# Levels issued in pairs in the recurrence phase, the last Fourier fold on GpSimd, and four smaller moves

## The reference

```python
def hybrid_mixer(h, w_in, w_fnet, lb_f, lb_b, out_norm, w_out):
    proj = h @ w_in                                    # 1024 -> 3072
    u, q, zf, zb, iv, g = jnp.split(proj, cuts, axis=-1)
    mixed = jnp.fft.fft2(ug, axes=(1, 3), norm="ortho").real      # 4 groups of 128
    y_fourier = jnp.einsum("blgc,gcd->blgd", mixed, w_fnet)
    k_f, logf_f = hgrn2_gates(zf, lb_f); k_b, logf_b = hgrn2_gates(zb, lb_b)
    o_fwd = chunked_gated_recurrence(qh, k_f, vh, logf_f)         # 4 heads of 128
    o_bwd = flip(chunked_gated_recurrence(flip(qh), flip(k_b), flip(vh), flip(logf_b)))
    y_rec = rms_norm(o_fwd + o_bwd, out_norm) * silu(g)
    return concatenate([y_fourier, y_rec]) @ w_out

def expert_choice_ffn(h, w_router, w_gate, w_up, w_down):
    affinity = softmax(xt @ w_router)
    g, idx = lax.top_k(affinity.T, cap)                # 16 experts, cap = tokens / 8
    he = silu(xe @ w_gate[e]) * (xe @ w_up[e]); ye = (he @ w_down[e]) * g
    return zeros.at[idx].add(ye)

x = x + hybrid_mixer(rms_norm(x, norm_mix), ...)
x = x + expert_choice_ffn(rms_norm(x, norm_ffn), ...)
return rms_norm(x, norm_final)
```

## Time and profile before

| what | us |
|---|---|
| median of 3 runs (2556.1 to 2558.35) | 2556.99 |
| the profiled execution's own time | 2552.32 |
| its span, first to last instruction | 2550.6 |
| PE busy in it | 2510.8 (98%) |
| DVE / ACT / POOL busy | 1648.6 (65%) / 1359.3 (53%) / 327.1 (13%) |
| mean granted TensorE clock | 0.997 |

### The profile page before, as it was taken

How to read it: one execution, slowest core, us unless ns; L and a number is a source line. 1 busy time by engine, 2 the same in 40 slices (tenths; PEclk the granted TensorE clock), 3 DMA queues, 4 the chain that set the end, 5 groups by cost and what they waited for, 6 DMA issues and landing times.

```text
span 2550.6 us, 44352 instructions
## 1 busy us (share of the span) xinstructions
PE 2510.8 (98%) x18109; PEld 2263.5 (89%) x18109; DVE 1648.6 (65%) x1997; ACT 1359.3 (53%) x1627; POOL 327.1 (13%) x237
## 2 busy tenths in 40 slices
PE   7999999999999999999999999999999999999998
PEld 6777778787877999999999999999999999999997
DVE  6556565444387676767667676766767666676667
ACT  6435353434665555555555555555555555555556
POOL 3102020101120011020211202021020202102020
PEclk9999999999999999999999999999999999999999
DMA  4001010135447676675767767676676767667677
GB/s 159 26 22 55 2 55 10 57 137 198 173 144 273 231 256 239 228 261 211 268 228 251 247 235 251 226 259 234 251 249 235 248 221 256 236 234 258 225 259 282
DMA packets 63987, 503.08 MB, mean 197 GB/s; under 512 B 7536, under 2 KB 7920, under 8 KB 39568
## 3 DMA queue, kind: packets, MB, share of 16 engines
q1 hardware_dynamic: 48016, 448.84, 48.3%
q0 software_dynamic: 15872, 52.83, 7.0%
HBM read 464.42 MB, written 37.22 MB: 197 GB/s over the span
## 4 chain that ended last, share of the span: by engine, by line
PE 92%; DVE 3%; ACT 2%; DMA 1%; issue 1%; POOL 0%; SPq 0%; DVEq 0%; ACTq 0%; POOLq 0%
PE up_banks_b L2241 15%; PE up_banks_a L2241 15%; PE up_banks_b L2244 6%; PE up_banks_a L2244 6%; PE bank L64 5%; PE bank L66 5%; PE bank L65 5%; PE up_banks_b L2282 2%; PE up_banks_b L2280 2%; PE up_banks_b L2281 2%; PE up_banks_b L2279 2%; PE up_banks_a L2283 2%; PE up_banks_b L2283 2%; PE up_banks_a L2279 2%; PE up_banks_a L2282 2%; PE up_banks_a L2280 2%
## 5 line engine op out<-in xcount | busy, mean ns | idle before, releaser
L2009 DVE TENSOR_TENSOR big_lo<-wide,big_hi 128x4096 fp32r<-128x4096 f32 x189 | 836.3, 4425 | 410.2 <-ACT big_hi L1774 410.0
L1774 ACT CAST big_hi<-wide 128x4096 fp32r<-128x4096 f32 x190 | 690.3, 3633 | 515.8 <-PE up_banks_a L2241 240.8
L2241 PE MATMUL up_banks_b<-x_parts,big_hi 128*128 128x384 f32 x2016 | 574.3, 356 | 0.0
L2241 PE MATMUL up_banks_a<-x_parts,big_hi 128*128 128x384 f32 x1984 | 565.0, 356 | 1.0 <-DVE h_parts L2033 1.0
L2244 PE MATMUL up_banks_b<-x_parts,big_lo 128*128 128x192 f32 x1764 | 442.0, 251 | 0.0
L2244 PE MATMUL up_banks_a<-x_parts,big_lo 128*128 128x192 f32 x1736 | 435.0, 251 | 0.0
L2241 PEld LDWEIGHTS up_banks_b<-x_parts,big_hi 128*128 128x128 f32 x2016 | 365.3, 189 | 0.2
L2241 PEld LDWEIGHTS up_banks_a<-x_parts,big_hi 128*128 128x128 f32 x1984 | 359.4, 189 | 1.9 <-DVE h_parts L2033 1.2
L2244 PEld LDWEIGHTS up_banks_b<-x_parts,big_lo 128*128 128x128 f32 x1764 | 336.1, 191 | 0.0
L2244 PEld LDWEIGHTS up_banks_a<-x_parts,big_lo 128*128 128x128 f32 x1736 | 330.8, 191 | 0.6
L64 PE MATMUL bank<-big_hi,w_hi 128*128 128x512 f32 x576 | 236.5, 411 | 0.0
(11 more groups left out here) (345 smaller groups left out, 4177.9 us busy)
## 6 DMA issues: line engine op xcount, KB each, us to landing
wide<-in_expert_weights SPq DMA_DIRECT2D x190, 2048.0 KB, 7.7
w_raw<-in_w_heads SPq DMA_DIRECT2D x48, 256.0 KB, 2.8
x_in<-in_x SPq DMA_DIRECT2D x12, 512.0 KB, 4.0
x_d<-in_x POOLq DMA_DIRECT2D x12, 512.0 KB, 5.8
residual<-x_d POOLq DMA_DIRECT2D x12, 512.0 KB, 3.6
ffn_in<-h_and_xT_d POOLq DMA_DIRECT2D x12, 512.0 KB, 3.0
wide<-residual SPq DMA_DIRECT2D x12, 512.0 KB, 6.4
tab<-in_tables POOLq DMA_DIRECT2D x10, 512.0 KB, 7.3
```

What stands on the lines that cost most here:

```text
L1774: nc.scalar.copy(ahead.hi(c), raw[:, c % RAW]).then_inc(hi_done, 1)
L2009: nc.vector.tensor_tensor(ahead.lo(c), raw[:, c % RAW], ahead.hi(c).bitcast(F32), ALU.subtract).then_inc(lo_done, 1)
L2241: last = nc.tensor.matmul(out[:, 0:2 * CAP], hi, x[:, k], start=n == 0, stop=n == KT - 1, skip_group_check=True)
```

## The change

1. **Heads, levels in pairs.** Levels 0 and 1, 2 and 3, 4 and 5, 6 and 7 are issued back to back on PE in the odd slots. For that the second level of a pair must not wait for a rise behind the first: a level with an even number reads copies of both its keys and its queries (`keys[0]` and the new buffer `queries`), an odd one a second buffer `keys[1]` and `kq`. ACT makes the copies in events of their own (`prep`), DVE rises once more as soon as they are made. Projections go into the slots as (1,2,1,2,1,2,1,0) halves, not (1,1,1,1,1,2,2,1): no half stands between level 7 and `intra`. The turn of v (`vt`) stands right before `intra`. `u` of the block before stands behind the half of slot 0 and directly ahead of the pair (0, 1). Updates and inters come one slot earlier; `rstd` moves to the front of its slot; where its `rows` stand at slot 7 they come behind `intra`. The copies of `near` into the scores are an event of their own (`near`) after `prep` of level 7.
2. **The last fold.** The sample's part of the fold of the last group goes from DVE to GpSimd (`fold_last`), behind GpSimd's last store of `u`.
3. **Kept sums.** ACT takes kept sums 0 and 1 behind the sixth of the eight w_out pieces, 2 behind the seventh and 3 behind the eighth.
4. **Weight piece.** The third early piece of L957 comes behind GpSimd's store of tile 10, not before that of tile 11.
5. **Prompt round.** Round 0 of the prompt's `take_best` goes from the end of the transform phase into the experts phase.
6. The program is built with `dynamic_dma_scratch_size=8192`.

```diff
+    BY_GPSIMD = (GROUPS - 1, 1)
+    def fold_rows(self, eng, on, g, part, done, count):
+        first, n = SEQS[part]
+        e, u = self.even[:, g, first // 2:(first + n) // 2], self.u[:, g, first:first + n]
+        on.tensor_copy(e[:, 0:1], u[:, 0:1]).then_inc(done, 1)
+        on.tensor_tensor(e[:, 1:], u[:, 1:n // 2], u[:, n - 1:n // 2:-1], ALU.add).then_inc(done, 1)
+        on.tensor_tensor(u[:, 1:n // 2], u[:, 1:n // 2], u[:, n - 1:n // 2:-1], ALU.subtract).then_inc(done, 1)
...
+    def fold_last(self, pool):
+        g, part = self.BY_GPSIMD
+        self.is_loaded(pool, g)
+        self.fold_rows(pool, self.nc.gpsimd, g, part, self.folded_last, 0)
...
-        keys = sb("keys", [P, BLK])
+        keys = [sb(f"keys{i}", [P, BLK]) for i in range(2)]
+        queries = sb("queries", [P, BLK])
...
-        FILL, LAST_FILL = (1, 1, 1, 1, 1, 2, 2, 1), (2, 2, 2, 1, 1, 1, 1, 1)
+        FILL, LAST_FILL = (1, 2, 1, 2, 1, 2, 1, 0), (2, 2, 2, 1, 1, 1, 1, 1)
...
-                    s = 1 + i // 2
+                    s = i // 2
                     at_slot[s] += [("update", h, d, k, turns[d][k]) for k in pair for d in range(2)]
                     at_slot[s + 1] += [("inter", h, d, k, turns[d][k + 1]) for k in pair for d in range(2)]
                 f = 2 + (steps - 1) // 2
                 at_slot[f] += [("square", h, b) for b in blocks]
                 at_slot[f + 1] += [("root", h, blocks[0])]
-                at_slot[f + 2] += [("rstd", h, blocks[0])]
+                at_front[f + 2] += [("rstd", h, blocks[0])]
...
             for s in range(8):
-                if n < NN:
-                    timeline.append(("level", n, s))
+                timeline += at_front[s]
+                if n < NN and s % 2 == 0:
+                    timeline.append(("prep", n, s + 1))
+                    if s == LEVELS - 1:
+                        timeline.append(("near", n))
+                elif n < NN:
+                    timeline += [("level", n, s - 1), ("level", n, s)]
+                    if s < LEVELS:
+                        timeline.append(("prep", n, s + 1))
+                if s:
+                    timeline += at_slot[s] + take_gates()
+                timeline += take_halves(FILL[s] if n < NN else LAST_FILL[s])
                 if s == 0 and n >= 1:
-                    timeline += [("u", n - 1, 0), ("u", n - 1, 1)]
-                timeline += at_slot[s] + take_gates()
-                timeline += take_halves(FILL[s] if n < NN else LAST_FILL[s]) + at_end[s]
+                    timeline += [("u", n - 1, 0), ("u", n - 1, 1)] + at_slot[0]
+                if s < 7 or n == NN:
+                    timeline += at_end[s]
             if n < NN:
-                timeline += [("intra", n), ("kt", n, 0), ("kt", n, 1)]
+                timeline += take_turn() + [("intra", n)] + at_end[7] + [("kt", n, 0), ("kt", n, 1)]
...
+                elif kind == "prep":
+                    _, n, s = ev
...
+                    if n >= 1 or s > 2:
+                        filled(act, ("level", n, s - 2) if s > 2 else ("level", n - 1, LEVELS + 1 - s))
+                    if s % 2 == 0:
+                        gather(queries, n, QB, QF, s - 1)
+                    gather(keys[s % 2], n, KF, KB, s - 1)
...
+                elif kind == "level" and ev[2] % 2 == 1:
                     _, n, s = ev
...
+                    rise(n, s)
+                    for t in (s - 1, s):
+                        take_level(("level", n, t))
+                elif kind == "prep" and ev[2] % 2 == 1 and ev[2] > 1:
+                    rise(ev[1], ev[2] - 1)
...
-    LOW_BETWEEN = {TT - 2: (0, 2), TT - 1: (4,)}
+    LOW_BETWEEN = {TT - 2: (0, 2)}
+    LOW_BEHIND = {TT - 2: (4,)}
...
-            act.wait_ge(wo_lo_done, KT)
-            for g in range(GROUPS):
+            def keep(g):
+                act.wait_ge(wo_lo_done, KT - 4 + g // 2 + 1)
                 act.wait_ge(y_filled, g + 1)
                 nc.scalar.copy(kept[:, g], banks[g][:]).then_inc(y_read, 1)
+            wo_high(range(KT - 2))
+            keep(0)
+            keep(1)
+            wo_high((KT - 2,))
+            keep(2)
+            wo_high((KT - 1,))
+            keep(3)
...
-            dve.wait_ge(aff_turned, 2)
-            take_best(then, nc, turned_lists, table, best, where, 2, 0, P_SLOTS)
+            ahead.aff_turned, ahead.turned_lists = aff_turned, turned_lists
...
-    nc = bacc.Bacc("TRN2", target_bir_lowering=False, num_devices=1)
+    nc = bacc.Bacc("TRN2", target_bir_lowering=False, num_devices=1, dynamic_dma_scratch_size=8192)
```

More of the change, by code:

```diff
@@ L495, in _ @@
                     pool.sem_inc(sig_used[i % 2], 1)
+            fourier.fold_last(pool)
         @block.scalar
@@ L512, in split_weights, with gather @@
                         weights.high(act, (h * NJ + j) * 2 + f)
-            def gather_keys(n, level):
-                if level == 0:
-                    act.wait_ge(kq_made, n + 1)
-                else:
-                    act.wait_ge(kq_up, n * LEVELS + level)
-                    filled(act, ("level", n, level))
-                if level == 0 and n >= 1:
-                    filled(act, ("level", n - 1, LEVELS))
+            def gather(out, n, left, right, level):
                 half = 1 << level
-                nc.scalar.copy(keys[:].rearrange("p (n two h) -> p n two h", two=2, h=half),
-                               halves(n % NB, KF, KB, level, 0, BLK)).then_inc(keys_ready, 1)
+                nc.scalar.copy(out[:].rearrange("p (n two h) -> p n two h", two=2, h=half),
+                               halves(n % NB, left, right, level, 0, BLK)).then_inc(keys_ready, 1)
             def take_projection(ev):
@@ L647, in sig_in, with rise, take_level @@
                 return sig[:, i % 2], sig_used[i % 2]
+            def rise(n, s):
+                nonlocal own
+                b, level = n % NB, s - 1
+                half = 1 << level
+                if level == 0:
+                    dve.wait_ge(kq_made, n + 1)
+                else:
+                    dve.wait_ge(kq_up, n * LEVELS + level)
+                pair = "p r (n two h) -> p r n two h"
+                products = decay[level][:].rearrange("p r (n two) -> p r n two", two=2)
+                shape = [P, 2, BLK // (2 * half), half]
+                right = kq[b][:, QF:KB + 1].rearrange(pair, two=2, h=half)[:, :, :, 1]
+                left = kq[b][:, KF:QB + 1].rearrange(pair, two=2, h=half)[:, :, :, 0]
+                up = decay[level + 1][:] if level + 1 < LEVELS else chunk_decay[:, b]
+                own += 1
+                nc.vector.tensor_tensor(up, products[:, :, :, 0], products[:, :, :, 1], ALU.mult).then_inc(dve_step, 1)
+                if s % 2 == 1:
+                    filled(dve, ("level", n, s))
+                else:
+                    prepared(dve, n, s)
+                own += 1
+                nc.vector.tensor_tensor(right, right, products[:, :, :, 0].unsqueeze(3).to_broadcast(shape), ALU.mult)\
+                    .then_inc(dve_step, 1)
+                nc.vector.tensor_tensor(left, left, products[:, :, :, 1].unsqueeze(3).to_broadcast(shape), ALU.mult)\
+                    .then_inc(kq_up, 1)
+            def take_level(ev):
+                _, n, s = ev
+                i = fill_of[ev][0]
+                if 1 <= s <= NEAR:
+                    filled(dve, ev)
+                    was_read(dve, ("level", n, s - 1))
+                    nc.vector.copy_predicated(near[:], mask[:, s - 1].unsqueeze(1).to_broadcast([P, CH, STRIP]),
+                                              near_view[i]).then_inc(bank_read[i], 1)
+                elif s == LEVELS:
+                    filled(dve, ev)
+                    dve.wait_ge(intra_done, n)
+                    nc.vector.tensor_copy(scores[P // 2:, :, 0:P // 2], bank[i][P // 2:, :, 0:P // 2])\
+                        .then_inc(bank_read[i], 1)
             norm.vector(dve)
@@ L1158, in _ @@
                     pool.dma_start(h_dram[row:row + P], h).then_inc(h_stored, 16)
+                    for k in ahead.LOW_BEHIND.get(s, ()):
+                        ahead.low_early(pool, nc.gpsimd, 1, slice(k, k + 2))
         @block.scalar
@@ L2055, in first_x_low @@
                     lows(r, first + r, hi_cols, lo_cols)
-            for slot in range(1, P_SLOTS):
-                take_best(choose, nc, table, table, best, where, 2, slot, P_SLOTS)
+            for slot in range(P_SLOTS):
+                if slot == 0:
+                    dve.wait_ge(ahead.aff_turned, 2)
+                take_best(choose, nc, table if slot else ahead.turned_lists, table, best, where, 2, slot, P_SLOTS)
                 if slot == X_SAMPLE_AFTER:
```

122 lines of the change are left out of this document (52 added, 70 removed).

## The result

The changed kernel takes 2598.9 us, median of four runs (2594.4 to 2603.5), against 2556.6 us (2554.2 to 2558.4): so 42 us slower by the medians; the ratio on record is 1.0175, 95% interval 1.0162 to 1.0187 (the quotient of the two medians is 1.0166, inside it). Forecast were 2582 us (+25), with a range up to 2598. The profiled execution of the changed kernel is the slowest of the four, 2603.5 us, and that of the kernel before (2552.3) is faster than all four of its runs. The two lie 51.2 us apart, 8.8 more than the medians. The four runs of the changed kernel go with their mean granted clock: 0.991 in the one of 2594.4 us, 0.990 and 0.989 in those of 2598.9, 0.988 in that of 2603.5.

A forecast was written before the change was run, and what follows sets the result against it. PE was taken to bound the kernel. Terms -15.4 + 17.7 + 11.2 + 14.5 + 0.5 - 3.0 = +25.5 us on the profiled 2552.3 gave 2577.8, plus 4.7 to the median, put at 2582; range 2556 to 2598.

The forecast's parts named there:

- Pairs: Heads, PE: two levels back to back pay the change of form once, 0.32 us saved a pair, 48 pairs, -15.4 us.
- Level 7 to intra: Heads: without a half between, PE waits for level 7's scores, 1.39 us in ten n, 1.9 in two, +17.7 us.
- Slots 5 to 7 of n = 3, 6, 9: Heads, counted from T, level 4's start: DVE and ACT late with rise, root and scores, PE waits 4.8 us each, +14.5.
- Level 1 behind u: Heads: level 1 waits for ACT's copy of u, whose bank it writes, longer behind table loads, +11.2 us.
- End of the heads: Block n = 11: u stands directly ahead of the inters that need it, +0.5 us.
- Transform and tail: Behind the heads: kept sums -1.6, fold 0, weight piece -0.85, prompt round -0.6, small scratch 0; together -3.0 us.
- the clock falls: Rival: in the heads, gaps in n = 3, 6, 9 drop PE's clock to half, +9 us, 2591; chance 0.17.
- Rival (a): Heads: nobody late but level 7, ACT and DVE finish root and copies nearly in time, 2557 to 2562 us; chance 0.18.
- (c): Rival: smaller DMA scratch makes GpSimd's DMA issues wait in the experts phase, 2597 with 1 us per expert; chance 0.05.
- (d): Rival: heads, pairs save more than the changes of form, 0.6 us a pair, -29 us, 2569; chance 0.12.

The follow-up runs named there:

- experiment 1: The changed kernel with extra 128x512 matmuls put on PE in all its waits ahead of intra, level 7 and level 1: 2589.7 us, ratio 1.0133.
- experiment 2: The changed kernel with extra matmuls only in the long waits, ahead of level 7 and intra in n = 3, 6, 9: 2597.5 us, ratio 1.0173.
- experiment 9: The kernel before with dynamic_dma_scratch_size=8192 and nothing else: 2553.7 us, ratio 1.0000.
- experiment 7: The kernel before with halves (1,1,1,1,1,2,3,0), so that no half stands between level 7 and intra: 2585.0 us, ratio 1.0125.

## Why the prediction was wrong

Its sign was right and its size was not: the median is 16.9 us above the forecast, and above the range. The waits came out nearly to the sum; what failed is the clock, which the sum had put at nothing, and after it the gain of the pairs.

**Pairs, -15.4.** Too high: -11.0. In a plain n it nearly held: n = 2 took 36.36 us from `intra` to `intra` before (137.98 to 174.34) and 36.65 now (142.31 to 178.96), with 1.44 us of waits; the rest is 1.15 us shorter, 0.29 a pair. But n = 4, 7 and 10 gave next to nothing; why is not shown. The bound of -13 allowed for `u` or an inter beside a level, and was not wide enough.

**Level 7 to intra, +17.7.** Held: PE waited 1.26 to 1.50 us in seven n and 1.85 in two, 12.8 us in all. With 1.3 for each of n = 3, 6 and 9 that is 16.7.

**Slots 5 to 7 of n = 3, 6, 9, +14.5.** Held: 2.84 for keys (three times), and 12.4 at `intra`, less the 3.9 already counted, 17.0. The steps came in the order written, and level 6 started at T + 9.1 as forecast (207.01, 216.09). But R, the end of the rise, came at 218.6, T + 11.6, 1.4 us behind its late end: L96 lay beside the rise. I had counted contention in the gates; it hit the rise and the 16-column product. So the keys of level 7 came late as well, and part of the wait stands there and not at `intra`. That the total is close to the forecast is in part luck: a later R, and then no more than 3.8 to 4.7 us at `intra` where 5 to 7 were forecast.

**Level 1 behind u, +11.2.** 8.6, less 0.9 of old waits: 7.7. The plain ones cost 0.2 and not 0.55; those with the table load 2.08, not 2.4.

**End of the heads, +0.5.** 1.4 us more of waiting for `state` at the inters, in three places.

**Transform and tail, -3.0.** -1.8 in this profile, -2.9 and a median of -2.5 with these edits alone. Contention of the fold with DVE did not show as a loss. Of the kept sums: no wait for them is left in the list.

**The step that failed is the clock.** The sum set it at nothing and made it a rival, "the clock falls", with a chance of 0.17 and +9 us, for three gaps of n = 3, 6, 9. It is no alternative to the forecast but follows from it: the waits forecast came to 43 us in a stretch that had one, and with them the clock went to 0.50 in eight stretches. It cost 17.9 us of work in the profiled execution, and experiment 1 shows it: with the waits filled by matmuls the clock is 1.00 and the heads end 13.6 us earlier, though PE has more to do. The places were wrong as well. The three gaps of the rival brought some 8 us, close to its 9; the other 10 came behind waits of 1.9 to 2.1 us, whose clock neither the sum nor the rival had counted (experiment 2).

In the profiles the sum now closes. The forecast was +25.5 against +51.2 measured, 25.7 apart: clock +17.9, pairs +4.4, first rows of x +1.5 (which the change does not touch), transform +1.2, experts +1.1, waits -0.5. In the medians the gap is 16.9, since the profiled execution of the changed kernel was 4.6 above its median and that of before 4.2 to 4.7 below. Part of that scatter is the clock again (0.988 in the profiled run, 0.989 to 0.991 in the others). How much of the median is the clock's is not measured; by these figures some 14 us, an estimate.

**Rival (a)** (nobody late) fell with the three waits of 3.8 to 4.7 us at `intra`, (c) with experiment 9, (d) with the -11.0 for 48 pairs.

## What to carry to other kernels

Putting two short steps side by side saves what lies between them, here 0.2 to 0.3 us a pair, and doubles the chain of work that must be ready before: price the chain (rises, copies, table loads) against the work that stays in between before counting the gain, and for every piece of cover that moves list all that it covered. When a forecast makes a busy TensorE wait, put the lower clock into the sum and not beside it. Test the parts of a bundle alone: the small edits here were worth 2.5 us, and the large one hid that.

## What the runs showed of the hardware

- The granted clock fell to 0.50 in eight stretches of a phase in which PE was otherwise always busy, and no length of wait divides the cases. In the heads it fell behind all waits of 2.8 us and more. Of those of 1.9 us nine left it at 1.00 in experiment 7, while it fell behind two of the same length in the changed kernel (528.6 and 566.2 us), and in experiment 2 once around 1.3 us. What decides is not shown here. "TensorE: Matmul & The Clock Gate" of the Trainium skill, section "HAM oscillation — how this bites in real kernels", tells of a kernel in which every wait for the next slice drops the clock again. This trace agrees for the waits in n = 3, 6 and 9, and shows falls behind shorter ones too.
- Matmuls into a bank that is overwritten later kept the clock up and made a kernel with more work faster (ratio 1.0133 against 1.0175).
- DVE beside GpSimd's L96: a product of 16 columns took 1.26 us (0.18 for its like in n = 6 of the kernel before), one of 512 columns 1.75 (0.69 alone). Both are stretched by about 1.1 us, so a small operation pays as much as a large one. It does not hit every one: in the heads of the changed kernel 25 products of 512 columns lay beside an L96, and 6 of them took 1.66 to 1.75 us.
